# Two kept passes, seven gathered ones, and other places for ada products, in a two-layer diffusion step

## What is computed

```python
hp = modulate(rmsnorm(xp, g_ffn[l]), mp[3], mp[4])
scores = jax.nn.sigmoid((t @ router_w).astype(jnp.float32))      # 16 experts in 4 groups
# the best group by its two best scores, then the top 2 experts inside it
wts = wts / jnp.sum(wts, axis=-1, keepdims=True)
hid = silu(einsum('td,edf->tef', t, w1)) * einsum('td,edf->tef', t, w3)   # f = 256
hid = hid * combine[:, :, None]
out = einsum('tef,efd->td', hid, w2)
xp = xp + mp[5] * out
```

## Time and profile before

| | us |
|---|---|
| median of three runs | 757.59 |
| the profiled execution | 760.02 |
| its span on the core | 758.2 |
| PE busy | 668.8 (88%) |
| DVE busy | 258.8 (34%) |
| ACT busy | 158.6 (21%) |
| POOL busy | 32.9 (4%) |

### The profile page before, as it was taken

The page is one execution under the profiler, slowest core; times in us unless marked ns, Lnnn a source line. Parts: engine busy times, 40 slices in busy tenths (PEclk is TensorE's granted clock), DMA queues, the critical chain, the costliest instruction groups (busy, mean ns, idle before and its releaser), DMA issues.

```text
span 758.2 us, 11297 instructions
## 1 busy us (share of the span) xinstructions
PE 668.8 (88%) x4744; PEld 343.4 (45%) x4744; DVE 258.8 (34%) x602; ACT 158.6 (21%) x314; POOL 32.9 (4%) x77
## 2 busy tenths in 40 slices
PE   4699999999999668999957989999996499999684
PEld 2555555557655343333312645566653233333142
DVE  0504668365612473131001440020525721211027
ACT  2301000254410231111101331131012311111023
POOL 1000000000000011000002000000000000000020
PEclk9999999999999879999979899999998789999897
DMA  8996030869964439999996795344844388999752
GB/s 367 379 429 258 31 138 1 331 274 426 425 271 167 166 129 397 380 405 424 425 429 238 323 420 232 136 176 188 332 168 166 138 322 318 408 427 425 322 194 84
DMA packets 27557, 213.65 MB, mean 282 GB/s; under 512 B 2768, under 2 KB 6640, under 8 KB 15856
## 3 DMA queue, kind: packets, MB, share of 16 engines
q1 hardware_dynamic: 17568, 182.06, 58.9%
q0 software_dynamic: 4320, 15.73, 5.8%
q10 hardware_dynamic: 5616, 15.09, 5.0%
HBM read 199.62 MB, written 13.25 MB: 281 GB/s over the span
## 4 chain that ended last, share of the span: by engine, by line
PE 79%; DVE 9%; DMA 4%; issue 3%; ACT 2%; POOL 0%; SPq 0%; POOLq 0%; DVEq 0%; ACTq 0%
PE bank L1435 28%; PE bank L1678 18%; PE bank L1693 8%; PE bank L1776 5%; PE bank L1369 3%; DMA ring<-in_ada_w 3%; DVE work L835 3%; PE bank L1488 2%; PE bank L1581 2%; DVE xT L838 2%; PE bank L1380 1%; DVE state L879 1%; PE bank L1659 1%; PE bank L1537 1%; PE bank L1748 1%
## 5 line engine op out<-in xcount | busy, mean ns | idle before, releaser
L1435 PE MATMUL bank<-state,ring 128*128 128x384 f32 x416 | 136.4, 487 | 1.2 <-ACT state L601 1.2
L1678 PE MATMUL bank<-ring,work 128*32 128x512 f32 x832 | 123.8, 635 | 14.9 <-issue 14.9
L1435 PEld LDWEIGHTS bank<-state,ring 128*128 128x128 f32 x416 | 78.2, 190 | 54.8 <-issue 2.3
L1435 PE MATMUL bank<-work,ring 128*128 128x384 f32 x256 | 83.4, 487 | 0.3 <-DVE work L835 0.3
L1435 PEld LDWEIGHTS bank<-work,ring 128*128 128x128 f32 x256 | 48.3, 190 | 35.0 <-DVE work L835 1.4
L1678 PEld LDWEIGHTS bank<-ring,work 128*32 128x32 f32 x832 | 31.4, 116 | 71.7 <-issue 71.6
L1693 PE MATMUL bank<-ring,work 128*32 128x512 f32 x416 | 58.1, 595 | 2.6 <-ACT work L721 2.6
L1229 DVE COPY work<-bank 128x512 f32<-128x512 f32 x18 | 12.4, 691 | 110.6 <-PE bank L1663 110.6
L838 DVE SCALAR_TENSOR_TENSOR xT<-bank,mod,xT 128x128 f32<-128x128 f32 x64 | 22.5, 411 | 73.9 <-PE bank L1435 67.1
L1776 PE MATMUL bank<-ring,state 128*128 128x512 f32 x96 | 41.6, 593 | 2.4 <-ACT state L601 2.4
L527 POOL DMA_INDIRECT work<-h_all,table x18 | 17.9, 992 | 595.7 <-DVE table L1089 461.0
(11 more groups left out here) (209 smaller groups left out, 731.4 us busy)
## 6 DMA issues: line engine op xcount, KB each, us to landing
ring<-in_moe SPq DMA_DIRECT2D x24, 2048.0 KB, 11.3
ring<-in_ada_w SPq DMA_DIRECT2D x12, 3072.0 KB, 14.7
ring<-in_moe SPq DMA_DIRECT2D x24, 1024.0 KB, 13.8
work<-in_ada_w SPq DMA_DIRECT2D x3, 3072.0 KB, 10.3
work<-in_moe SPq DMA_DIRECT2D x4, 2048.0 KB, 11.5
state<-in_moe SPq DMA_DIRECT2D x4, 2048.0 KB, 12.9
y_slots<-work ACTq DMA_DIRECT2D x16, 512.0 KB, 9.5
ring<-in_gm_in SPq DMA_DIRECT2D x4, 2048.0 KB, 17.3
```

Source lines behind the costliest of these rows:

```text
L1435: mm = pe.matmul(ps[:, 0:T], w[:, k, j * P:j * P + P], x[:, k, :], start=(k == 0), stop=(k == KD - 1))
L1678: mm = pe.matmul(bank[p % 2][rows, :], h_slotT[:, p % 2, k * P + BLOCK * n:k * P + BLOCK * n + BLOCK], held(place_of(e))[:, k * 512:k * 51 ...
```

## The change

The two last passes are kept on the chip instead of one (KEPT_PASSES), so that seven passes are stored and the gathers wait for the seventh store. `moe_add` multiplies both with their own matrix in last_wT, and has its loop over d outside. Scale and sum of the gathered rows (`scaled`, `summed`) come in the round of the last pass, ahead of the copies of its rows. The 32-place experts become sixth and seventh, the 96-place one eighth, so that the last two passes hold experts 12 to 15 and LATE (experts 5 and 11) is free after the seventh pass. Product 11 goes ahead of router 0, product 15 ahead of router 1, product 12 into the norm before the gated MLP, and 13 and 14 take the places of 14 and 15. Product 15 is loaded to SPARE before the experts 2 to 4 of layer 1. The load of gm_in 0 waits for the first product of moe_add. SP reads the number of each sorted expert right before its load. A dummy Exp follows the root of norms 1 and 3. The shares (the last four operations of `route`, which normalise the two scores to combine) become `shares` and are called behind `order_experts`. The diff, with what belongs to `experts_all` and to places of constants left out:

```diff
...
 BLOCK = 32
-CAPS = [96] * 6 + [64] * 8 + [32] * 2
 FIXED = SLOTS + 1
+RANKS = [10, 9, 0] + list(range(1, 9))
+CAPS = [96] * FIXED + [([96] + [64] * 8 + [32] * 2)[rank] for rank in RANKS]
...
 PASSES = PLACES // P
-STORED = (PASSES - 1) * P
+KEPT_PASSES = 2
+STORED = (PASSES - KEPT_PASSES) * P
...
 TABLES = ((0, PLACE_AT[FIXED] // P), (PLACE_AT[FIXED] // P, PASSES))
-RUNS = [(4, 1), (5, 1), (6, 8), (14, 2)]
+RUNS = [(4, 1), (5, 2), (7, 1), (8, 8)]
...
           + [("ada", n) for n in range(5, 11)] + [("ev_out", c) for c in range(2)] + [("ada", 11)]
-          + [("moe", (0, e)) for e in range(NE)] + [("ada", 12), ("ada", 13), ("gm_in", 0), ("gm_in", 1), ("ada", 14), ("gm_in", 2)]
-          + [("ada", 15), ("gm_in", 3)] + [("gm_out", c) for c in range(2)] + [("moe", (1, e)) for e in range(NE)])
+          + [("moe", (0, e)) for e in range(NE)]
+          + [("ada", 12), ("gm_in", 0), ("ada", 13), ("gm_in", 1), ("ada", 14), ("gm_in", 2), ("gm_in", 3)]
+          + [("gm_out", c) for c in range(2)] + [("ada", 15)] + [("moe", (1, e)) for e in range(NE)])
...
         place = i[1] % HELD if kind == "moe" else 0
-        s = SPARE if kind == "ada" and 11 <= i <= 13 else place if place >= SLOTS else (r + place) % SLOTS
+        s = SPARE if kind == "ada" and i in (11, 12, 15) else place if place >= SLOTS else (r + place) % SLOTS
...
+HEAD_ADA = (11, 15)
+
+
 def dispatch_products(l):
-    return ([("router", l), ("logits", l)] + [("h_row", l, t, c) for t in range(NT) for c in range(2)]
-            + [("slots", l), ("table", l, 0)])
+    return ([("ada_row", HEAD_ADA[l]), ("router", l), ("logits", l)] + [("h_row", l, t, c) for t in range(NT) for c in range(2)]
+            + [("ada_t", HEAD_ADA[l]), ("slots", l), ("table", l, 0)])
...
     + [("mix_out", 0, d) for d in range(KD)] + [("norm", 1)]
-    + dispatch_products(0) + [("ada_row", 11), ("ada_t", 11), ("ada_row", 12), ("ada_t", 12)]
-    + [("moe_t", 0, d) for d in range(KD)] + [("norm", 2), ("ada_row", 13)]
-    + [("gm_v", t, 0) for t in range(NT)] + [("ada_row", 14), ("ada_t", 13)] + [("gm_v", t, 1) for t in range(NT)]
-    + [("ada_t", 14)] + [("gm_u", j) for j in range(4)] + [("ada_row", 15)] + [("gm_u", j) for j in range(4, 6)]
-    + [("ada_t", 15)] + [("gm_u", j) for j in range(6, KD)] + [("spatial", g) for g in range(KD)]
+    + dispatch_products(0)
+    + [("moe_t", 0, d) for d in range(KD)] + [("norm", 2), ("ada_row", 12)]
+    + [("gm_v", t, 0) for t in range(NT)] + [("ada_row", 13), ("ada_t", 12)] + [("gm_v", t, 1) for t in range(NT)]
+    + [("ada_row", 14), ("ada_t", 13)] + [("gm_u", j) for j in range(4)] + [("ada_t", 14)]
+    + [("gm_u", j) for j in range(4, KD)] + [("spatial", g) for g in range(KD)]
...
         s_own = carve(NT * SORTED)
-        last_w = carve(NT, P)
-        last_wT = carve(T)
+        last_wT = carve(KEPT_PASSES, T)
...
         all_rows = h_rows
+        all_w = ring[:, 0, :]
...
             .rearrange("p (t n) -> p t n", t=NT)
+        last_w = work[:, at[0]:at[0] + NT * PLACES // 2].rearrange("p (t n) -> p t n", t=NT)[:, :, 0:KEPT_PASSES * P]
+        assert KEPT_PASSES * P <= STORED // 2
...
                 kind, i = key
-                if key == ("ada", 13):
-                    sp.wait_ge(s_sum[0], NT)
+                if key == ("gm_in", 0):
+                    b, turn = bank_of(("moe_t", 0, 0))
+                    sp.wait_ge(full[b], turn + 1)
...
             def load_up(l, j):
+                if j >= FIXED:
+                    place_expert[l, j] = sp.value_load(order_i[0:1, l, j - FIXED:j - FIXED + 1], min_val=0, max_val=NE - 1)
...
                     sp.wait_ge(full[b], turn + 1)
-                    load("ada", 11)
-                for j in (2, 3, 4) if l == 0 else (4, 2, 3):
+                else:
+                    sp.wait_ge(s_sg, KD)
+                load("ada", HEAD_ADA[l])
+                for j in (2, 3, 4):
...
                 sp.wait_ge(s_order, l + 1)
-                for j in range(FIXED, NE):
-                    place_expert[l, j] = sp.value_load(order_i[0:1, l, j - FIXED:j - FIXED + 1], min_val=0, max_val=NE - 1)
...
                 for b in range(2):
-                    pool.wait_ge(s_yst[l][b], 16 * len(range(b, PASSES - 1, 2)))
+                    pool.wait_ge(s_yst[l][b], 16 * len(range(b, PASSES - KEPT_PASSES, 2)))
...
                 take(act.activation(dst, product(*key)[:, 0:T], ACT.Sqrt, bias=eps[:, 0:1]), *key)
+
+            def load_exp():
+
+                act.activation(sm_sum[:, 0, 3:4], eps[:, 0:1], ACT.Exp)
...
                 act.activation(silu[:, p % 2, :], bank[p % 2][:, 0:F], ACT.Silu).then_inc(s_silu[l], 1)
+
+            def scaled(l):
+
+                act.wait_ge(s_weight, 2 * l + 2)
+                for t in range(NT):
+                    act.wait_ge(s_back[l][0][t], 16)
+                    act.activation(moe_out[:, t, :], moe_out[:, t, :], ACT.Identity, scale=weight[:, l, 0, t:t + 1])\
+                        .then_inc(s_scaled[l], 1)
...
                         copy_h(l, p + 2)
+                    if p == PASSES - 1:
+                        scaled(l)
...
                     act.activation(y_slot[:, b, 0:512], bank[4][:, :], ACT.Identity).then_inc(s_y0[l], 1)
-                    if p == PASSES - 1:
-                        break
+                    if p >= PASSES - KEPT_PASSES:
+                        continue
...
-                if l == 0:
-                    ada(12)
-
-                act.wait_ge(s_weight, 2 * l + 2)
-                for t in range(NT):
-                    act.wait_ge(s_back[l][0][t], 16)
-                    act.activation(moe_out[:, t, :], moe_out[:, t, :], ACT.Identity, scale=weight[:, l, 0, t:t + 1])\
-                        .then_inc(s_scaled[l], 1)
-
...
                 take(act.activation(logit_t[:, :], product("router", l)[:, 0:T], ACT.Identity), "router", l)
+                ada(HEAD_ADA[l])
...
             root(rstd[:, :], "norm", 1)
+            load_exp()
...
             dispatch(0)
-            ada(11)
...
             modulate(2)
-            ada(13)
+            ada(12)
...
                          "gm_v", t, c)
-                if c == 0:
-                    ada(14)
+                ada(13 + c)
...
                 take(act.activation(uT[:, j, :], product("gm_u", j)[:, 0:T], ACT.Gelu), "gm_u", j)
-                if j == 3:
-                    ada(15)
...
             root(rstd[:, :], "norm", 3)
+            load_exp()
...
                 step(dve.tensor_reduce(s_rank[:, :], square(s_ahead), AX.X, ALU.add))
-                step(tt(square(s_at), each_column(place_no[:, 0:SORTED]), each_row(s_rank[:, :]), ALU.is_equal))
+                step(tt(square(s_at), each_column(ranks[:, :]), each_row(s_rank[:, :]), ALU.is_equal))
...
                 order_experts(l)
+                shares(l)
...
                 step(dve.tensor_reduce(s_own[:, :].rearrange("p (t j) -> p t j", t=NT), cube[1], AX.X, ALU.add))
+                ada(HEAD_ADA[l])
...
                 dve.wait_ge(s_w8t, l + 1)
-                dve.tensor_copy(last_wT, bank[7][:, P:P + T]).then_inc(s_w8T, 1)
+                for i in range(KEPT_PASSES):
+                    dve.tensor_copy(last_wT[:, i, :], bank[4 + i][:, 0:T]).then_inc(s_w8T, 1)
...
                 tt(hidden[:, p % 2, :], silu[:, p % 2, :], bank[p % 2][:, F:2 * F], ALU.mult).then_inc(s_hid[l], 1)
+
+            def summed(l):
+                for t in range(NT):
+                    dve.wait_ge(s_scaled[l], t + 1)
+                    dve.wait_ge(s_back[l][1][t], 16)
+                    stt(moe_out[:, t, :], second[:, t, :], weight[:, l, 1, t:t + 1], moe_out[:, t, :],
+                        ALU.mult, ALU.add).then_inc(s_sum[l], 1)
...
                         gate(l, p + 1)
+                    if p == PASSES - 1:
+                        summed(l)
...
                         index_rows(l)
-                if l == 0:
-                    ada(12)
...
                     experts_all(l)
-                for t in range(NT):
-                    dve.wait_ge(s_scaled[l], t + 1)
-                    dve.wait_ge(s_back[l][1][t], 16)
-                    stt(moe_out[:, t, :], second[:, t, :], weight[:, l, 1, t:t + 1], moe_out[:, t, :],
-                        ALU.mult, ALU.add).then_inc(s_sum[l], 1)
...
             dispatch(0)
-            ada(11)
...
             norm(2)
-            ada(13, 14)
+            ada(12, 13)
...
                 stt(v_rows[:, t, :], v_rows[:, t, :], ss[:, 3 + t:4 + t], v_gain, ALU.mult, ALU.mult).then_inc(s_vn, 1)
-            ada(15)
+            ada(14)
...
-
+                ada_rows(HEAD_ADA[l])
...
                         closed(mm, "h_row", l, t, c)
+                ada_turned(HEAD_ADA[l])
...
                 pe.wait_ge(s_w8, len(KEPT) * (l + 1))
-                for t in range(NT):
-                    tr = pe.transpose(bank[7][:, P + t * P:P + t * P + P], last_w[:, t, :], ident[:, :])
+                for i in range(KEPT_PASSES):
```

(60 more changed lines are left out.)

3 lines of the change are left out of this document (1 added, 2 removed).

## The result

The changed kernel took 769.11 us in the median of four runs (766.14 to 771.79), the kernel before 756.85 (755.75 to 759.02). The ratio is 1.016, 95% interval 1.011 to 1.020: slower by about 12 us. The profiled execution of the changed kernel took 771.79 us with a span of 770.0, against 760.02 and 758.2: 11.8 us more.

The account below looks back on a forecast made before the run. PE carries most of the chain, with DMA full in the passes. Terms +3.3 (layer 0), +0.5 and +6.6 (layer 1) and 0.3 (register reads) gave +10.7 us, 768.3 on the median of 757.6; range 757 to 775.

Parts of the forecast that it names:

- serial PE work behind the gathers: End of each layer: it costs more than earlier gathers and shorter stalls give back; the forecast itself, chance 0.62.
- Landing to root: From the last gather's landing to the norm's root, all serial: 28.6 us in layer 0, 27.2 in layer 1.
- the clock: PE, idle before moe_add, starts its products at the lower clock: 2.2 us more, bounds 0 and 2.9.
- Landing: When the last gather lands at the layer's end: about 411 us in layer 0, 727.7 in layer 1.
- the conserved bytes: Layer 0's gathers queue behind the ada load: 3.15 MB at about 420 GB/s, 7.5 us more after 403.
- Stalls: PE's waits for weights before the last pass fall from 8.63 and 6.24 us to about 3 us each.
- expert 4: In layer 0 its load waited for product 11; now some 20 us earlier, so layer 0 loses its lag.
- Head: Router to first pass in each mixture layer: about -0.2 us in layer 0, +0.5 in layer 1.
- Product 12: Moves from layer 0's end, where the gathers were said to hide it, into the norm's gap: 0.
- B: Rival at the layers' ends: gathers undisturbed by weights and PE not slow; down to 756 us, half 762; chance 0.20.
- C: Rival at the layers' ends: gathers land before the last pass ends, shorter stalls become gain; 750 us; chance 0.07.
- D: Rival in the passes: pass 7 gets its weights late, 3 us per layer; 774 us; chance 0.11.

Follow-up runs that it names:

- e1: Changed kernel, both passes kept, but last-pass copies ahead of scale and sum and moe_add's products ahead of the wait for the sums: 753.53 us.
- e2: Changed kernel with the end-of-layer order undone and one pass kept instead of two: 747.29 us, ratio 0.987 to the kernel before.
- e3: Changed kernel with one pass kept and its serial end-of-layer order left in place: 773.75 us, ratio 1.023 to the kernel before.
- e9: Kernel before with only the new order of the experts (32-place sixth and seventh, 96-place eighth): 753.89 us, ratio 0.994.
- e10: Changed kernel with one pass kept, the end-of-layer order undone and the experts in the old order: 752.72 us, ratio 0.996.
- e8: Changed kernel with SP's eleven register reads in one batch again: 770.71 us in one execution.
- e6: Changed kernel without the dummy Exp behind the root of norms 1 and 3: 771.74 us in one execution.
- e7: Changed kernel with only the copies of the last pass's rows put back ahead of scale and sum: 765.87 us, ratio 1.013.
- e4: Changed kernel with the 3 MB load of ada product 12 issued only after moe_add's first product: 762.58 us, ratio 1.007.
- e5: Changed kernel with unused extra PE products behind the last pass, 16 in layer 0 and 7 in layer 1: 766.70 us, ratio 1.012.

## Why the prediction was right, step by step

**The sum.** 768.3 us were forecast and 769.1 measured; +10.7 and +11.8 in the profiled executions. The likeliest case, serial PE work behind the gathers, is what e1, e2 and e3 show. That the sum fits to 1 us is partly luck: layer 0 came out 1.3 us dearer than forecast (+4.6, not +3.3), layer 1's end 2.9 cheaper, and 2.8 us fell where nothing was forecast.

**Landing to root.** 28.6 and 27.2 us were predicted, 28.1 and 26.4 measured. (The terms as listed add up to 28.8 and 27.4.) The parts: sum 1.3 us, then 2.48 and 2.21 to the first product, of which 0.6 are the end of DVE's copy and 1.90 and 1.62 register read and branch, moe_add 18.6 and 17.6 (417.79 to 436.40, 737.27 to 754.88), norm 5.2. Predicted were 2.99 and 1.58 for the branch, 1.1 too much in layer 0: the 2.99 us before were PE's whole idle time, in which DVE still worked on product 12. For moe_add 18.1 was predicted in both, with 2.2 for the clock; the clock cost about 2.9 and 1.9. PE was idle for 14.5 and 6.5 us before moe_add; some 10 and 5 had been given as the sign.

**Landing.** In layer 0 411 was predicted, 413.55 measured. 1.3 us of this are pass 7's later end; the conserved bytes gave 18.5 us from the first issue instead of 20.3; and the start at 392.5 was 0.5 us too early for its own rows (382.55 + 0.8 + 8.9, and 0.8 from landing to the first gather, as counted in layer 1). In layer 1 24.3 us from pass 7's end were predicted, 22.2 measured. The start of the gathers matched, 10.0 us predicted and 9.8 measured (711.45 to 721.28); the gathers did not: 13.0 us and 1.4 for the weights still in flight were predicted, 12.4 in all measured (721.28 to 733.67). The term for the weights was too much, so that layer 1's end, forecast at +6.6, came to +3.7.

**Stalls.** Both at about 3 us: 3.86 and 3.76. Right in size; its cause was only half right, since I put part of layer 0's gain on expert 4 (e9, e10). That the shorter stalls bring nothing in the changed kernel held: the chain leaves PE at pass 7's end.

**Head.** -0.2 and +0.5 were predicted, with the first passes; measured +0.4 (-1.3 and +1.7) and +0.6. The first half pass of layer 0 took 6.35 us instead of 5.27, the upper bound of what I had allowed. That this is the moved product 11 isn't shown: in the ten traces with the new head the same instructions took 4.86 to 6.42 us, in the two with the old one 5.27. The transposes cost 0.3. Reads: 0 (e8). Exp: 0.3 to 0.5 us (e6), not the 2.7 that the Trainium skill (ScalarE: Activation LUTs, What ACT_TABLE_LOAD costs) would give.

**Product 12.** The prediction held that the gathers hid it at the end of layer 0, and that of the identity products only the last third waits for the last gather. In layer 0 neither was so: product 12 delayed moe_add, and the end of the layer cost 5.6 us more than without it (e10). This didn't spoil the forecast, since layer 0's new root was added up from the landing and not from what product 12 had cost. But it is why landing to root grew by only 13.4 us in layer 0, against 17.3 in layer 1, and a good part of what e2 gains.

**What was not in the sum.** 0.9 us before layer 0's router, where nothing was changed (261.9 to 264.4 us in the twelve traces), and 1.9 between root and router of layer 1. Of the latter 1.7 are the first 48 products of the gated MLP: 22.54 us instead of 20.84. Of twelve traces six show 20.8 (before, e1, e2, e3, e7, e9) and six 22.5 (after, e4, e5, e6, e8, e10). The ten with the new code ahead are of both kinds, so that code alone doesn't decide it; the old form is in two traces only, both 20.8, too few to call it the same. The forecast's error in layer 1's end and these terms cancel by chance.

**Rivals.** B (gathers undisturbed, PE not slow) was true for layer 1's gathers only. C (gathers before the last pass ends) is nearly so in layer 1, the last gather landed at 733.7, and the last products of the last pass ended at 730.8 (PE is idle from there for 6.46 us in the timeline), and even there 26 us of work behind them remain; what e1 changes is that work. D (weights late in the middle) did not come: no wait before passes 5 to 7.

## What to carry to other kernels

When a wait is shortened, list what was running under it. Here PE could do the products of the kept rows while the gathers ran; put behind them, they cost more than the whole wait had shrunk. Look at what stands first in an engine's queue at such a place: product 12 was taken for hidden and cost 5.6 us (e10). A transfer that is not urgent belongs behind the gathers that the chain waits for (e4), and the order in which weights are needed can shorten a bandwidth-bound wait with no byte less (e9).

## What the runs showed of the hardware

- A 3 MB load issued 9 us ahead of six 0.5 MB gathers, on another queue, delayed the last of them by 7.4 us, which is all of its own bytes at 425 GB/s (e4).
- PE's register read and branch before moe_add took 1.90 and 1.62 us from the end of the last copy in the changed kernel, after 14.5 and 6.5 us of idling, and 1.98 and 1.76 in e1, where PE had just worked. It doesn't shrink when PE is busy before it.
- After the wait for weights before the last pass, 3.4 to 3.9 us long in ten kernels, the next 32 instructions took 3.64 us in seven cases, 5.34 in seven and 6.15 to 6.40 in six. In the changed kernel (3.64, both layers) the granted clock stayed at 1.00, in e7's layer 1 (6.29) it was 0.50 right behind the wait. The length of the wait doesn't sort them; the same idle time cost nothing or 2.7 us.
- Whether TensorE falls to the lower clock at the start of the gated MLP (a mean of 0.64 in its first 2.6 us in the changed kernel, 1.00 in e1), after an idle time of 2.1 to 2.4 us behind busy stretches, changes from execution to execution (20.8 or 22.5 us for the same 48 instructions, each in six traces) and is worth 1.7 us. What decides it is open; no run was made for it.
